# One unit for the half-filled last gate and factor columns of four FFNs, and 8 warming products in place of 50

## What is computed

```python
D_FF = 2752
def rmsnorm(x, g):
    y = x * lax.rsqrt(jnp.mean(x * x, axis=-1, keepdims=True) + EPS)
    return y * g
def adaln_in(x, g, m, i):
    return rmsnorm(x, g) * (1 + m[:, i, 1][:, None]) + m[:, i, 0][:, None]
def swiglu(h, w1, w3, w2):
    return (jax.nn.silu(h @ w1) * (h @ w3)) @ w2
cond = jax.nn.silu(c)
for l in range(DEPTH):                                   # DEPTH = 2
    m = (cond @ w_mod[l] + b_mod[l]).reshape(bsz, 3, 3, D_MODEL)
    x = x + 0.5 * m[:, 0, 2][:, None] * swiglu(adaln_in(x, norm_g[l, 0], m, 0), ffn_w1[l, 0], ffn_w3[l, 0], ffn_w2[l, 0])
    h = adaln_in(x, norm_g[l, 1], m, 1) @ w_in[l]
    ...                                                  # attention and convolution: mix
    x = x + m[:, 1, 2][:, None] * (mix @ w_out[l])
    x = x + 0.5 * m[:, 2, 2][:, None] * swiglu(adaln_in(x, norm_g[l, 2], m, 2), ffn_w1[l, 1], ffn_w3[l, 1], ffn_w2[l, 1])
```

## Time and profile before

| what | us |
|---|---|
| median of 3 runs (lowest, highest) | 1497.18 (1495.74, 1497.48) |
| the profiled execution: its time | 1500.95 |
| the profiled execution: span of the trace | 1499.0 |
| PE busy in the span | 1436.5 (96%) |
| DVE busy | 1092.0 (73%) |
| ACT busy | 699.0 (47%) |
| mean DMA rate | 206 GB/s |

### The profile page before, as it was taken

How to read it: one execution, slowest core, us unless ns; L and a number is a source line. 1 busy time by engine, 2 the same in 40 slices (tenths; PEclk the granted TensorE clock), 3 DMA queues, 4 the chain that set the end, 5 groups by cost and what they waited for, 6 DMA issues and landing times.

```text
span 1499.0 us, 26571 instructions
## 1 busy us (share of the span) xinstructions
PE 1436.5 (96%) x11012; PEld 1353.3 (90%) x11012; DVE 1092.0 (73%) x1831; ACT 699.0 (47%) x1125; POOL 24.8 (2%) x24
## 2 busy tenths in 40 slices
PE   3999999999999999999999999999999899899998
PEld 3999998889999999999988699999996669799998
DVE  6788898777777879878667766565683676586776
ACT  3333536444434354344464343434564765555543
POOL 0000000000000000000000000000010030000000
PEclk9999999899999999999999999999996899999999
DMA  9996957236777568567533046565322204345552
GB/s 393 387 386 247 364 211 276 87 133 269 289 284 305 195 261 329 230 243 303 217 127 113 29 169 239 211 227 182 141 85 99 104 23 145 123 169 189 192 177 77
DMA packets 32183, 308.25 MB, mean 206 GB/s; under 512 B 3480, under 2 KB 5784, under 8 KB 7360
## 3 DMA queue, kind: packets, MB, share of 16 engines
q1 hardware_dynamic: 32064, 306.56, 53.0%
HBM read 305.48 MB, written 1.06 MB: 205 GB/s over the span
## 4 chain that ended last, share of the span: by engine, by line
PE 90%; DVE 5%; ACT 2%; issue 1%; DMA 1%; SPq 0%; DVEq 0%; ACTq 0%
PE bank L833 14%; PE bank L658 13%; PE bank L662 13%; PE bank L659 13%; PE bank L750 7%; PE bank L752 7%; PE bank L757 6%; PE bank L628 3%; DMA X<-in_x 1%; PE bank L903 1%; PE bank L619 1%; PE bank L676 1%; PE bank L914 1%; DVE WL L1776 1%; PE bank L734 1%
## 5 line engine op out<-in xcount | busy, mean ns | idle before, releaser
L1776 DVE TENSOR_TENSOR WL<-ring,WH 128x1024 fp32r<-128x1024 f32 x418 | 500.2, 1222 | 46.1 <-ACT WH L1235 43.8
L1235 ACT ACTIVATE WH<-ring 128x1024 fp32r<-128x1024 f32 x418 | 427.8, 1054 | 126.9 <-PE bank L833 55.3
L658 PE MATMUL bank<-XH,WH 128*128 128x256 f32 x1680 | 409.3, 282 | 1.4 <-ACT WH L1235 1.4
L659 PE MATMUL bank<-XL,WH 128*128 128x256 f32 x1680 | 407.7, 281 | 0.0
L658 PEld LDWEIGHTS bank<-XH,WH 128*128 128x128 f32 x1680 | 316.2, 188 | 7.1 <-issue 5.5
L659 PEld LDWEIGHTS bank<-XL,WH 128*128 128x128 f32 x1680 | 316.2, 188 | 0.5 <-issue 0.5
L662 PE MATMUL bank<-XH,WL 128*128 128x256 f32 x1680 | 233.8, 282 | 1.0 <-DVE WL L1776 1.0
L662 PEld LDWEIGHTS bank<-XH,WL 128*128 128x128 f32 x1680 | 213.9, 188 | 1.2 <-DVE WL L1776 1.2
L1315 ACT ACTIVATE SG<-bank 128x256 f32<-128x256 f32 x88 | 33.8, 384 | 376.2 <-PE bank L662 358.7
L750 PE MATMUL bank<-GH,WH 128*128 128x256 f32 x840 | 202.5, 279 | 0.7 <-ACT WH L1235 0.7
L752 PE MATMUL bank<-GL,WH 128*128 128x256 f32 x840 | 202.4, 279 | 0.0
(11 more groups left out here) (318 smaller groups left out, 1656.4 us busy)
## 6 DMA issues: line engine op xcount, KB each, us to landing
ring<-in_stream SPq DMA_DIRECT2D x132, 1536.0 KB, 6.6
scr<-in_stream SPq DMA_DIRECT2D x15, 1536.0 KB, 9.9
PR<-in_stream SPq DMA_DIRECT2D x15, 1536.0 KB, 8.5
att<-in_stream SPq DMA_DIRECT2D x15, 1536.0 KB, 10.4
ring<-in_stream SPq DMA_DIRECT2D x9, 1024.0 KB, 5.0
ring<-in_stream SPq DMA_DIRECT2D x10, 512.0 KB, 3.6
kf_mix<-in_stream SPq DMA_DIRECT2D x2, 1536.0 KB, 15.9
con<-in_consts SPq DMA_DIRECT2D x1, 2000.0 KB, 17.0
```

Source lines behind the costliest of these rows:

```text
L658: pe.matmul(o, part(WH, u, k), XH[:, k, :], start=(k == 0), stop=False)
L659: pe.matmul(o, part(WH, u, k), XL[:, k, :], start=False, stop=False)
L1235: act.activation(part_all(WH, u), raw(u), ACT.Copy).then_inc(*mark("high", u))
L1776: dve.tensor_tensor(part_all(WL, u), raw(u), part_all(WH, u).bitcast(F32), ALU.subtract)\
```

## The change

**Half units.** For the feed-forwards 0 to 3, the last chunk (21) has one unit instead of two in the stream: its left 64 columns are the last 64 gate columns, its right 64 the last 64 factor columns. PE runs one unit of 24 matmuls, which puts the gate on partitions 0 to 63 of the bank and the factor on partitions 64 to 127. ACT writes Silu of the first to partitions 64 to 127 of `SG`; DVE multiplies, and splits, on partitions 64 to 127 only. In `w2` of that chunk the 64 real rows now lie below 64 rows of zeros. The item shrinks from 1536 to 1024 KB. All later units count one less per feed-forward, so ACT and DVE, which split a fixed number of units ahead, reach one unit further in chunk 20: the first unit of the next stage is split there, ahead of Silu of chunk 21.

**The start.** Behind the sums of the first norm come 3 warming products, 3 after the root of the sums (`stat_root`), and 2 after `ada_in`: 8 in place of 50. At the start of every feed-forward ACT and DVE split up to unit 3 (`up_units(f, 1)[1]`) ahead of Silu 0 and of the first gated product. On DVE, for the first feed-forward, this stands ahead of the last two rows of mod 5.

```diff
@@ -88,6 +88,11 @@
 MOD_SLOT, MODS_OF, MOD_ROW_AT, WIN_MODS = mod_plan()
+def half_chunk(f, c):
+
+    return f < 4 and c == NFF - 1
+
+
 def stream_plan():
@@ -97,7 +102,7 @@
     def ffn(f):
         for c in range(NFF + 1):
-            names = [("w1", f, c), ("w3", f, c)] if c < NFF else []
+            names = [("w1", f, c)] if half_chunk(f, c) else [("w1", f, c), ("w3", f, c)] if c < NFF else []
             names += [("w2", f, c - 1)] if c > 0 else []
             items.append((("ffn", f, c), UNIT * len(names)))
             units.extend((n, ("ffn", f, c), UNIT * k) for k, n in enumerate(names))
@@ -293,6 +298,8 @@
         name = UNITS[u][0]
         if name[0] in ("w1", "w3", "w2"):
+            if name[0] == "w1" and half_chunk(*name[1:]):
+                return "ffn_up", *name[1:]
             if name[0] == "w2" and name[2] == NFF - 1:
                 return "ffn_out", name[1], KD - 1
             return {"w1": "w1_used", "w3": "ffn_up", "w2": "ffn_down"}[name[0]], *name[1:]
@@ -509,7 +516,8 @@
         return UNIT_AT[name, 0]
     def up_units(f, c):
-        return UNIT_AT["w1", f, c], UNIT_AT["w3", f, c]
+        u = UNIT_AT["w1", f, c]
+        return (u, u) if half_chunk(f, c) else (u, UNIT_AT["w3", f, c])
     def scaled(k, c):
@@ -651,7 +659,8 @@
                     take(4 + c % 2, *(("g32", f, c) if f < 4 else ("up_conv", c)))
                     if c == 0:
                         return first_up(b)
-                    for a, u in enumerate(up_units(f, c)):
+                    merged = half_chunk(f, c)
+                    for a, u in enumerate(up_units(f, c)[:1] if merged else up_units(f, c)):
                         o = b[:, a * S:(a + 1) * S]
                         pe.wait_ge(*at("high", u))
                         for k in range(KD):
@@ -660,7 +669,7 @@
                         pe.wait_ge(*at(*low_of(u)))
                         for k in range(KD):
                             last = pe.matmul(o, part(WL, u, k), XH[:, k, :], start=False, stop=(k == KD - 1))
-                        last.then_inc(*mark("w1_used" if a == 0 else "ffn_up", f, c))
+                        last.then_inc(*mark("w1_used" if a == 0 and not merged else "ffn_up", f, c))
                 def first_up(b):
@@ -1025,9 +1034,11 @@
             pe.wait_ge(*at("ones_in"))
             norm(("sub", 0, 0))
-            for i in range(2, HEAD_MODS):
-                pe.wait_ge(*(at("mod_read", i) if i < HEAD_MODS - 1 else at("ada_in", 0, 0)))
-                keep_warm(14 if i < HEAD_MODS - 1 else 8)
+            keep_warm(3)
+            pe.wait_ge(*at("stat_root", ("sub", 0, 0)))
+            keep_warm(3)
+            pe.wait_ge(*at("ada_in", 0, 0))
+            keep_warm(2)
             for l in range(2):
                 ffn(2 * l)
                 a = "ac"[l]
@@ -1297,7 +1308,7 @@
                 return lambda c: [("x_added", stage, c)]
             def ffn(f):
-                split_to(up_units(f, 0)[1])
+                split_to(up_units(f, 1)[1])
                 for c in range(NFF):
                     act.wait_ge(*at("ffn_up", f, c))
                     if f == 4:
@@ -1312,8 +1323,11 @@
                         act.wait_ge(*at("up_conv_g", c))
                     if c >= 2 and f < 4:
                         act.wait_ge(*at("g32", f, c - 2))
-                    act.activation(SG[:, c % 2, :], guc[:, c % 2, 0, :] if f == 4 else bank[4 + c % 2][:, 0:S], ACT.Silu)\
-                        .then_inc(*mark("silu", f, c))
+                    if half_chunk(f, c):
+                        act.activation(SG[64:P, c % 2, :], bank[4 + c % 2][0:64, 0:S], ACT.Silu).then_inc(*mark("silu", f, c))
+                    else:
+                        act.activation(SG[:, c % 2, :], guc[:, c % 2, 0, :] if f == 4 else bank[4 + c % 2][:, 0:S], ACT.Silu)\
+                            .then_inc(*mark("silu", f, c))
                     split_to(up_units(f, c)[1] + PARTS)
                     if f == 0:
                         start_step(c)
@@ -1895,16 +1909,17 @@
                         dve.wait_ge(*at("up_conv", c))
                         second = guc[:, c % 2, 1, :]
                     else:
-                        second = bank[4 + c % 2][:, S:2 * S]
+                        second = bank[4 + c % 2][64:P, 0:S] if half_chunk(f, c) else bank[4 + c % 2][:, S:2 * S]
                     dve.wait_ge(*at("silu", f, c))
                     if c >= 1:
                         dve.wait_ge(*at("gated", f, c - 1))
-                    dve.tensor_tensor(G32, SG[:, c % 2, :], second, ALU.mult).then_inc(*mark("g32", f, c))
+                    h = slice(64, P) if half_chunk(f, c) else slice(0, P)
+                    dve.tensor_tensor(G32[h], SG[h, c % 2, :], second, ALU.mult).then_inc(*mark("g32", f, c))
                     dve.wait_ge(*at("g32", f, c))
                     if c >= 2:
                         dve.wait_ge(*at("ffn_down", f, c - 2))
-                    link(dve.tensor_copy(GH[:, c % 2, :], G32))
-                    dve.tensor_tensor(GL[:, c % 2, :], G32, GH[:, c % 2, :].bitcast(F32), ALU.subtract)\
+                    link(dve.tensor_copy(GH[h, c % 2, :], G32[h]))
+                    dve.tensor_tensor(GL[h, c % 2, :], G32[h], GH[h, c % 2, :].bitcast(F32), ALU.subtract)\
                         .then_inc(*mark("gated", f, c))
                     ends = f < 4 and c == NFF - 1
                     if not ends:
@@ -2120,6 +2135,7 @@
             for l in range(2):
                 if l == 0:
                     norm_parts_of(("sub", 0, 0), lambda: split_to(up_units(0, 0)[1]))
+                    split_to(up_units(0, 1)[1])
                     dve.wait_ge(*at("gate_rows_in"))
                     for r in range(1, MOD_ROWS):
                         mod_row(HEAD_MODS - 1, r)
@@ -2515,8 +2531,12 @@
         F = NFF * P
         a, b = chunked(padded(w1, D, F)), chunked(padded(w3, D, F))
         c = padded(w2, F, D).reshape(NFF, P, D)
+        if n < 4:
+            half = F - P
+            a[:, NFF - 1] = chunked(np.concatenate([w1[:, half:], w3[:, half:]], 1))[:, 0]
+            c[NFF - 1] = np.concatenate([np.zeros((64, D), np.float32), w2[half:]], 0)
         for j in range(NFF + 1):
-            rows = [a[:, j].reshape(P, -1), b[:, j].reshape(P, -1)] if j < NFF else []
+            rows = [a[:, j].reshape(P, -1), b[:, j].reshape(P, -1)][:1 if half_chunk(n, j) else 2] if j < NFF else []
             blocks["ffn", n, j] = np.concatenate(rows + ([c[j - 1]] if j else []), 1)
     def proj(name, w, per=3):
```

## The result

| | us |
|---|---|
| before, median of 12 runs (lowest, highest) | 1492.06 (1486.73, 1499.07) |
| after, median of 12 runs (lowest, highest) | 1484.43 (1479.16, 1489.81) |
| ratio after / before, 95% interval | 0.9947 (0.9922 to 0.9973) |
| forecast | 1487.2, range 1483.8 to 1491.2, 10.0 us less |
| span of the profiled execution, before and after | 1499.0 and 1482.9 |

The change makes the kernel 7.9 us faster (0.53%, from the means; the medians differ by 7.6 us), with 4.0 to 11.6 us inside the interval. The difference is 2 us less than forecast, but the interval holds the forecast. The time 1484.43 lies inside the range, 0.6 us above its lower end, and this is in part luck: the median before, with more runs, lies 5.1 us under the one from which the forecast was taken.

What follows compares the result with a forecast made beforehand. PE was taken as the bound, holding 90% of the chain that ended last. Half units 7.87, units 2 and 3 1.7 and the start 0.4 summed to 10.0 us: 1497.18 - 10.0 = 1487.2, range 1483.8 to 1491.2.

Steps and rivals of the forecast that it cites:

- The half units: Ends of feed-forwards 0 to 3: chunk 21's product comes earlier by DVE's idle time, at most 2.79 us each; sum 7.87.
- one of the signs of being wrong: Prediction wrong if first differences at 74 us exceed 1.5 us, or a feed-forward's end gains less than DVE's idle.
- idle of rows 3: DVE's idle time before the gated product of chunk 21: 1.29, 1.49, 2.30 and 3.53 us in feed-forwards 0 to 3.
- the rival that ended slower: Before Silu 21, ACT blocks on the next stage's first load, landing in 11.3 us; time 1500.8, chance 0.04.
- Units 2 and 3 at once: Starts of feed-forward 2 and the last: PE's waits of 1.0 and 0.7 us go; 1.7 us gained.
- The start: Kernel start: 7.3 us won on PE, 6.9 given back in waits for items 2 and 4; 0.4 us stays.
- my inner bound of -0.2: Start's gain if item 4 lands 3.65 us late; the outer bound put 1 us on DVE being late below that.
- the whole list of SP behind item 2: Kernel start: bias, positions, item 3, large constants, mod 8 and item 4, all issued 4.45 us later with item 2.
- the other half of the same argument: Load queue at the start stands empty from 45.7 to 48.1, so item 4 lands at least 2.4 us later; 3.0 taken.
- The clock rival: Clock falls at the start's new waits for items 2 and 4, costing 0.1 to 4 us; time 1489.7, chance 0.16.
- 1.9 us of cover: PE's wait for item 4, 72.2 to 74.1 us, hides that much of a half clock after the first wait.
- The loads did not keep up: Rival for the start: queue absorbs item 2's late issue, start worth up to 3.45 us; time 1484.2, chance 0.13.

Runs made afterwards that it cites:

- the start alone: Changed kernel with full units in chunk 21, keeping 8 warming products and the early split of units 2 and 3; ratio 0.9979 (0.995 to 1.0007) to before.
- rows first: Changed kernel with DVE's two rows of mod 5 ahead of the low parts of units 2 and 3; Silu of chunk 5 at 87.53 us.
- warming alone: Kernel before with 8 warming products in place of 50, rows of mod 5 where they were; Silu of chunk 5 at 85.32 us.

## Why the prediction held, step by step

**The half units: mechanism right, size nearly.** The forecast was 1.29, 1.49, 2.30 and 2.79, sum 7.87. Found: 1.26, 1.34, 2.13 and 2.8, sum 7.5. The product of chunk 21 came earlier by DVE's idle time, less 0 to 0.2. By the letter, one of the signs of being wrong came true, that an end gains less than the idle of rows 3, by 0.03 to 0.17 us; the bound was drawn without any margin. The price of a unit was read a little low: the 172 matmuls in 20.00 us count those that only touch the stretch, and the distance of 8.51 us from Silu to Silu, a chunk of 72 matmuls, makes it 2.84 us and not 2.79. That the missing part lies behind modulation rows is shown by the run without them. The next stage's first load never held ACT: the rival that ended slower didn't come.

**Units 2 and 3 at once.** Forecast 1.0 and 0.7, found 1.2 and 0.8, nothing in feed-forwards 1 and 3.

**The start.** Forecast: 7.3 us on PE, of which 0.4 stay. Found: PE began chunk 1 6.4 us earlier. (The 7.3 didn't fit the forecast's own start of chunk 1 at 43.3, which is 5.5 us earlier; it isn't in the sum.) Silu of chunk 5 stands at 88.74, 88.57 and 89.85 in the three profiles with the new start (after twice, and the start alone) against 88.85, 88.03 and 87.97 in three with the old one; by the means the start costs 0.8 us where 0.4 were to be won. With spreads of 1.3 and 0.9 us in three profiles each, even the sign is not certain. It lies under my inner bound of -0.2. The times of the forecast's chain were right: item 2 issued at 47.17 (forecast 48.1; item 1 landed 1.0 earlier in this run, at 41.3), ready at 54.17 (54.4), item 4 at 72.92 (73.1), chunk 4 begun at 74.13 (74.1). One link was not, that the whole list of SP behind item 2, with item 4 at its end, is issued later. Item 4 was issued 2.1 us earlier, and only the empty queue, the other half of the same argument, moved its landing. That chunk 4 began at the forecast's 74.1 is in part chance, as the next paragraph shows. What I had not seen is that the start before is itself not fixed: the eight sums take 6.25 us in the first profile, 5.54 and 5.35 in the other two with the old start, and all behind them moves with them (chunk 1 at 48.77, 47.97 and 47.90). The single products of these sums stand 0.43 us apart at first and 0.22 later; the step comes at 29.0 us in the first profile and at 27.7 in the second, though the clock column reads 1.00 from 24 us on in both.

**The clock rival took place, and cost 0 to 1.1 us.** The prediction named a granted clock of 1.00 from 55 on as something the profile would show, and that was wrong in all three profiles with this start. After the wait at 51.4 to 55.4 the clock fell, as the rival said. Here are three stretches of after:

```profile
52.00:54.00 2.00, 0.00 (x0) 0.00 (x0) 0.00 (x0) 0.00 (x0) 0.00 (x0) 1.00 0.92 256
56.00:58.00 2.00, 2.00 (x11) 2.00 (x11) 2.00 (x4) 1.39 (x2) 0.00 (x0) 0.50 1.05 447
58.00:60.00 2.00, 2.00 (x15) 2.00 (x15) 1.93 (x5) 0.00 (x0) 0.00 (x0) 0.77 1.00 427
```

`up(2)` took 7.4 us instead of 5.9, so 1.6 us more. I had counted on 1.9 us of cover for it, the wait for item 4, and that is what it used. The high part for chunk 4 was ready at 72.92 + 1.06 = 73.98, and PE came at 74.13, without a wait; in the second profile of after PE waited 0.39 us. In the run with the start alone the clock stayed down longer, `up(2)` took 8.5 us, and 1.1 us were left over that nothing covered. So the rival's mechanism is there, at the low end of its 0.1 to 4 us. The rule of the Trainium skill (TensorE: Matmul & The Clock Gate, "What's actually happening"), that the throttled state is the default and activity releases it, agrees with these rows; what it cost was decided by the loads. In the run with rows first, where the load came earlier, it cost 1.4 us.

**The sum.** 7.5 + 2.0 - 0.8 = 8.7 us by stages, forecast 10.0, measured 7.9 (4.0 to 11.6). The loads did not keep up (item 4 landed 2.8 us later), so that this rival's time is nearest to the measured one is chance. The term of the sum that was off is the start, by 1.2 us. The rest of the 16.1 us between the first two profiles lies in the attentions, and two profiles of one program differ there by as much. Why the clock falls at other moments there from run to run stays open; only that it does is shown.

## What to carry to other kernels

Taking work off the bottleneck engine gained here no more than the idle time that the next engine in the chain had ahead of its part; read that idle time off the row before counting removed instructions. At the start of a program that streams its weights, follow an edit to the landing of the next loads: of 6.4 us won on PE, about half could not last in either order, as item 4 landed no earlier, and the other half (2.7 to 3.5 us in the run with warming alone) went because two reductions that free a buffer moved behind other work. And where the clock falls at other moments from run to run, compare stages, not spans.

## What the runs showed of the hardware

A gap of PE of 2.09 us, in a feed-forward of otherwise dense matmuls, was followed by a granted clock of 0.75, 0.50 and 0.90 in the three stretches from 72 to 78 us and cost 1.4 us; with 8 products of ones in the gap it stayed at 1.00. The waits of 3.5 to 4.3 us for item 2 were followed by a fall in all four profiles that have them. But shorter gaps and light work went either way. A gap of 1.42 us ahead of chunk 1 left the clock at 1.00 in all three profiles with the old start, and the same gap in the run with warming alone, behind products with pauses, was followed by 0.50 from 44 to 46. And from 33.5 to 37 us, where PE works on the chunks of XH in eight pairs of matmuls 0.40 us apart, the clock fell to 0.50 in both profiles of after and in the start alone, and stayed at 1.00 in the run with rows first, whose program is the same up to there. So no length of a gap that is safe can be read from these runs.

One program on one core, undisturbed, varied from 1486.7 to 1499.1 us; in its two profiles the variation lay in the attention stages and went with the granted clock.
